# Feed-forward heads over two pairs of row blocks, projection tails by token thirds, and three operand sums on GpSimd

## The reference, cut to what matters

```python
x = x + mix
h = rms_norm(x, norm_ffn[layer])
proj = einsum('btd,df->btf', h, w_in)             # 1024 -> 2 x 2816
a, gate = proj[..., :D_FF], proj[..., D_FF:]
full = concatenate([conv_hist, a], axis=1)
conv = conv_b + sum(full[:, j:j + T] * conv_w[j] for j in range(3))
y = einsum('btf,fd->btd', gelu(conv) * gate, w_out)   # 2816 -> 1024
x = x + y
```

## Time and profile before

| | us |
|---|---|
| median of 3 runs (lowest, highest) | 2767.11 (2763.37, 2767.15) |
| the profiled execution's own time | 2769.66 |
| its span | 2767.9 |
| TensorE busy | 2653.7 |
| VectorE busy | 1843.3 |
| ScalarE busy | 935.5 |
| GpSimd busy | 397.6 |

### The profile page before, as it was taken

One profiled execution on the slowest core, in us unless ns is written; L12 is line 12 of the kernel. 1 busy time (PEld: TensorE's weight loads), 2 busy tenths in 40 slices (PEclk: granted clock), 3 DMA queues, 4 the chain that ended last, 5 costly groups with the idle time before them and its releaser, 6 DMA issues.

```text
span 2767.9 us, 45361 instructions
## 1 busy us (share of the span) xinstructions
PE 2653.7 (96%) x17812; PEld 2579.9 (93%) x17812; DVE 1843.3 (67%) x3057; ACT 935.5 (34%) x1546; POOL 397.6 (14%) x303
## 2 busy tenths in 40 slices
PE   9999999699999998999999999999599999999997
PEld 8989999599999998999888999999599999999997
DVE  3658983687677777789223754454777777777787
ACT  4424462333232233345222112113432222333343
POOL 3234325101010110000001230012101111110000
PEclk9999999799999999999999999999799999999999
DMA  4111001222222338533111111111222222348533
GB/s 149 38 35 54 24 24 38 102 64 72 72 81 69 109 126 288 189 123 118 36 61 50 35 43 42 42 42 34 99 68 91 64 81 72 107 140 291 172 126 126
DMA packets 232449, 248.98 MB, mean 90 GB/s; under 512 B 13051, under 2 KB 170436, under 8 KB 232004
## 3 DMA queue, kind: packets, MB, share of 16 engines
q1 hardware_dynamic: 232228, 246.36, 27.2%
q10 hardware_dynamic: 32, 0.01, 0.0%
HBM read 202.12 MB, written 44.20 MB: 89 GB/s over the span
## 4 chain that ended last, share of the span: by engine, by line
PE 84%; DVE 9%; issue 3%; DMA 2%; ACT 1%; SPq 0%; DVEq 0%; POOL 0%; POOLq 0%; ACTq 0%
PE banks L1420 34%; PE banks L1453 14%; PE banks L917 10%; PE banks L1495 7%; PE banks L942 5%; PE banks L1073 3%; PE banks L1359 2%; PE banks L966 2%; DMA fraw<-in_w_out_ffn 1%; PE banks L1108 1%; PE banks L1011 1%; DVE xs L2076 1%; DVE xs L2229 1%; PE banks L1555 1%; DVE qsc L1734 1%
## 5 line engine op out<-in xcount | busy, mean ns | idle before, releaser
L1420 PE MATMUL banks<-cx,fh 128*128 128x288 f32 x2816 | 497.0, 299 | 44.0 <-DVE cx L2103 33.7
L1420 PEld LDWEIGHTS banks<-cx,fh 128*128 128x128 f32 x2816 | 419.3, 192 | 48.8 <-ACT cx L2978 26.2
L1420 PE MATMUL banks<-cw,fh 128*128 128x288 f32 x2112 | 364.2, 294 | 2.1 <-DVE cw L2103 2.1
L1420 PEld LDWEIGHTS banks<-cw,fh 128*128 128x128 f32 x2112 | 307.7, 188 | 2.5 <-issue 2.5
L1420 PE MATMUL banks<-cx,fl 128*128 128x288 f32 x1408 | 305.8, 298 | 0.0
L1453 PE MATMUL banks<-ysh,fh 128*128 128x288 f32 x1232 | 267.7, 299 | 21.0 <-DVE ysl L2209 20.4
L1453 PE MATMUL banks<-ysh,fl 128*128 128x288 f32 x1232 | 266.5, 298 | 0.0
L1453 PE MATMUL banks<-ysl,fh 128*128 128x288 f32 x1232 | 265.8, 297 | 0.0
L3410 POOL TENSOR_TENSOR gate<-gate,cv 128x1152 f32<-128x1152 f32 x44 | 119.9, 2725 | 953.9 <-DVE gate L2128 788.7
L1420 PEld LDWEIGHTS banks<-cx,fl 128*128 128x128 f32 x1408 | 229.9, 192 | 0.0
L1420 PE MATMUL banks<-cw,fl 128*128 128x288 f32 x1056 | 225.6, 294 | 0.0
(11 more groups left out here) (382 smaller groups left out, 5371.3 us busy)
## 6 DMA issues: line engine op xcount, KB each, us to landing
fraw<-in_w_out_ffn SPq DMA_DIRECT2D x264, 256.0 KB, 3.2
fraw<-in_w_in_ffn SPq DMA_DIRECT2D x176, 256.0 KB, 4.0
y_scratch<-gate SPq DMA_DIRECT2D x44, 576.0 KB, 2.8
raw<-in_w_uv_c SPq DMA_DIRECT2D x64, 256.0 KB, 2.8
yb<-y_scratch SPq DMA_DIRECT2D x10, 1440.0 KB, 9.3
raw<-in_w_in_ab SPq DMA_DIRECT2D x40, 256.0 KB, 2.9
x_scratch<-xs SPq DMA_DIRECT2D x16, 576.0 KB, 7.2
xs<-x_scratch SPq DMA_DIRECT2D x4, 2304.0 KB, 12.1
```

The source lines that it names most:

```text
L1420: mm = pe.matmul(bank[:, M0 + c * CH:M0 + (c + 1) * CH], w[:, pos % RING, k * P:(k + 1) * P], x[:, m, part, c * CH:(c + 1) * CH], start=fi ...
```

## The change

- **Tail by thirds.** Planes 6 and 7 in layer 0, planes 4 to 7 in layer 1 are computed third by third (`by_token_block`). Their weight parts lie in `tw_h`, `tw_l` (freed space), their squares in eight places `sq_t`. `norm_block` 0 stands before the last group of the second third, 1 after the first group of the last third, 2 after the first head product; blocks 1 and 2 take the last plane's square by a second matmul without the GpSimd sum.
- **Head over two pairs.** Pairs 0 and 1 run side by side, q = 1, 2, 3, 7, 5, 6, 4 for both, in four bank pairs, with new places `p1b`, `d1`, `a1`. VectorE's and ScalarE's orders are written out anew; weight sums are formed in place. Step 0's convolution comes at products 13 to 16.
- **Residual later.** Stores of the tail planes are split: first two thirds, then the last. `xs` planes 0 to 3 are read back at down steps 13 and 15 instead of 10; `yb12` is read at steps 22 and 26 instead of 13 and 15, `yb21` at 34, 38, 40 instead of 24, 26, 28. SP's queue issues the weight blocks of pairs 0 and 1 and the stores before the small history loads.
- **Turn to down.** The low parts of steps 0 and 1 come before the last eviction, and the last three convolution parts come in steps 1 to 3; the last gelu comes at step 4 instead of 2.
- **Sums on GpSimd.** `y_sum` for q = 1, 6, 7 (33 of 55 steps a layer) is done by GpSimd after its last `y_prod`; q = 3, 4 stay on VectorE.

```diff
-PLAN.add("abo", 16, 24, 32)
+PLAN.add("abo", 16, 24, 30)
...
+        HEAD = tuple((n, q) for q in (1, 2, 3, 7, 5, 6, 4) for n in range(2))
...
+                sp.wait_ge(acc_free, g0 + NTB * first + 2 * (KD - first))
+                for d in range(first, KD):
+                    sp.dma_start(xscr[l][d][:, 0:2 * TB], xs[:, d, 0:2 * TB]).then_inc(x_moved, 16)
+                sp.wait_ge(acc_free, g0 + NTB * KD)
+                for d in range(first, KD):
+                    sp.dma_start(xscr[l][d][:, 2 * TB:TOK], xs[:, d, 2 * TB:TOK]).then_inc(x_moved_late, 16)
...
-                    if r == 10:
-                        sp.wait_ge(x_moved, 160 * l + 144)
-                        sp.dma_start(xs[:, 0:4, :], xscr[l][0:4].rearrange("d p t -> p d t")).then_inc(x_moved, 16)
+                    if r in (13, 15):
+                        d = r - 13
+                        sp.wait_ge(x_moved, 176 * l + 144)
+                        sp.dma_start(xs[:, d:d + 2, :], xscr[l][d:d + 2].rearrange("d p t -> p d t"))\
...
-                    if r in (13, 15):
-                        a, b = ((0, 6), (6, 11))[r // 15]
+                    if r in (22, 26):
+                        a, b = ((0, 6), (6, 11))[r // 26]
                         y_tiles(yb12[:, a:b, :], a, b, T2S, y_back[1])
-                    if r in (24, 26):
-                        a, b = ((0, 5), (5, 10))[r // 26]
+                    if r in (34, 38):
+                        a, b = ((0, 5), (5, 10))[r // 38]
                         y_tiles(yb21[:, a:b, :], STEPS + a, STEPS + b, T1S, y_back[0])
-                    if r == 28:
...
+            def by_token_block(l, group, ssq):
+
+                first = TAIL_D[l]
+                for tb in range(NTB):
+                    for d in range(first, KD):
+                        if tb == 1 and d == KD - 1:
+                            norm_block(l, 0, ssq)
+                        group(d, tb)
+                        if tb == 2 and d == first:
+                            norm_block(l, 1, ssq)
+
+            def norm_block(l, tb, ssq):
+
+                k = 1 + 2 * l
+                bank = ps[6 + (tb == 0)][:, 0:TB]
+                pe.wait_ge(ssq_added, tail_added(l, tb))
+                if tb == 2:
+                    pe.wait_ge(rms_ready, NTB * k + 2)
+                mm = pe.matmul(bank, ones[:, :], ssq[:, tbs(tb)], start=True, stop=tb == 0)
+                if tb:
+                    s = tail_square(l, KD - 1, tb)
+                    pe.wait_ge(square_ready, TAKEN_SQ[l] + s + 1)
+                    mm = pe.matmul(bank, ones[:, :], sq_t[:, s % 8, :], start=False, stop=True)
+                mm.then_inc(norm_mm, 1)
+
             def norm(k, ssq, blocks=range(NTB)):
 
-                pe.wait_ge(ssq_added, SQUARES[k])
...
+            for u in range(2, 6):
+                abo_unit(n0 + 2 * u, g0 + 3 * u, n0 + 2 * u, g0 + 3 * u)
+
+            def abo_group(d, tb):
+
+                e = 18 + 2 * tb + d - 6
+                acc_bank(g0 + e, g0 + e)
+                for h, (rh, rl) in enumerate(((oh, ol), (ph, pl))):
+                    pe.wait_ge(w_high_ready, n0 + 2 * d + h + 1)
+                    pe.wait_ge(w_low_ready, n0 + 2 * d + h + 1)
+                    for k in range(4):
+                        for c, (w, r) in enumerate(((tw_h, rh), (tw_h, rl), (tw_l, rh))):
+                            mm = pe.matmul(ps[(g0 + e) % BANKS][:, 0:TB], w[:, 2 * (d - 6) + h, k * P:(k + 1) * P],
+                                           r[:, k, tbs(tb)], start=h == k == c == 0, stop=h == 1 and k == 3 and c == 2)
+                mm.then_inc(pe_tick, 1)
+            by_token_block(0, abo_group, ssq_e)
...
+                def head_product(pos):
+
+                    n, q = HEAD[pos]
+                    pe.wait_ge(f_high, done + pos + 1)
+                    pe.wait_ge(f_low, done + pos + 1)
+                    if q == 1:
+                        pe.wait_ge(acc_free, g0 + 20 + 2 * n)
+                    if q == 2:
+                        pe.wait_ge(up_act_out, head_act(l, n, "p1"))
+                    if q == 3:
+                        pe.wait_ge(acc_free, g0 + NTB * KD)
+                        if n:
+                            pe.wait_ge(rms_ready, NTB * (2 + 2 * l))
+                            pe.wait_ge(convc_ready, l + 1)
+                    if q == 7:
+                        pe.wait_ge(up_act_out, head_act(l, n, "c11"))
+                    if q == 5:
+                        pe.wait_ge(up_act_out, head_act(l, n, "e3"))
+                    if q == 6:
+                        pe.wait_ge(up_dve_out, head_dve(l, n, "d"))
+                    if q == 4:
+                        pe.wait_ge(up_dve_out, head_dve(l, n, "c22"))
+                    passes(pos, psp[n + (2 if q in (3, 5) else 0)], q, q in (1, 3, 7, 5))
+
...
+                turn_taps()
+                for pos in range(14):
+                    head_product(pos)
+                    if pos == 0:
+                        norm_block(l, 2, ssq_b if l else ssq_e)
+                for n in range(2, PAIRS):
                     for j in range(7):
                         product(n, j)
...
+                def at_first(tb, d0, d1):
+
+                    for d in range(d0, d1):
+                        (down_tail if l else abo_tail)(d, tb)
...
+                dve.wait_ge(rstd_ready, NTB * 2 * l + 2)
+                dve.wait_ge(x_moved, 176 * l + 16 * KD)
                 for d in range(4):
                     normed(d, T1S)
+                at_first(2, KD - 1 - l, KD - 1)
+                combo_low(0, 0)
+                combo_low(0, 1)
+                at_first(2, KD - 1, KD)
+                combo_low(0, 2)
+                combo_low(0, 3)
+                normed(4, T1S)
+                normed(5, T1S)
+                combo_low(2, 0)
+                normed(6, T1S)
+                combo_low(2, 1)
+                normed(7, T1S)
+                combo_low(2, 2)
+                combo_low(2, 3)
+                up_low(3)
+                dve.wait_ge(rstd_ready, NTB * (1 + 2 * l))
+                dve.wait_ge(x_moved_late, 96 if l else 32)
+                for d in range(4, KD):
+                    normed(d, T2S)
+                dve.wait_ge(convc_mm, l + 1)
                 for k in range(4):
+                    combo_low(6, k)
+                up_sum(4)
+                up_low(4)
+                for d in range(4):
+                    normed(d, T2S)
+                combo_sum(4, 2)
+                up_sum(5)
+                up_low(5)
                 for k in range(4):
+                    combo_sum(3, k)
+                for k in range(4):
+                    combo_low(3, k)
+                for pos in (6, 7):
+                    up_sum(pos)
+                    up_low(pos)
+                for k in (0, 1, 3):
+                    combo_sum(4, k)
+                for k in range(4):
+                    combo_sum(1, k)
+                for k in range(4):
+                    combo_low(4, k)
+                for n in range(2):
+                    head_evict(n, "d")
+                    up_low(8 + n)
+                for k in range(4):
+                    combo_sum(5, k)
+                for k in range(4):
                     combo_low(1, k)
+                for n in range(2):
+                    head_evict(n, "a")
+                    up_low(10 + n)
+                for k in range(4):
+                    combo_low(5, k)
+                up_low(12)
+                up_low(13)
                 dve.memset(apad_a[:, 0:2], 0.0)
                 dve.memset(apad_b[:, 0:2], 0.0)
+                up_evict(10)
...
                     j, kk = divmod(r, STEPS)
                     q = DOWN_ORDER[j]
-                    if q not in SUMMED_Y:
+                    if q not in SUMS_ON_DVE:
                         return
-                    if kk == 0 and q == 1:
-                        dve.wait_ge(y_back[0], 64 * l + 16)
-                        dve.wait_ge(y_back[1], 64 * l + 32)
-                        dve.wait_ge(y_back[2], 48 * (l + 1))
-                    elif kk == 0:
+                    if kk == 0:
+                        dve.wait_ge(ys_summed, 5 * STEPS * l + sums_of(r, SUMMED_Y) - 1)
                         dve.wait_ge(y_back[q == 3], 64 * (l + 1))
                     a, b = Y_PARTS[q]
                     dve.wait_ge(f_done, done + UPS + r - 3)
                     dve.tensor_tensor(yslf[:, r % RINGD, :], y_block(a, kk), y_block(b, kk),
-                                      ALU.subtract if q in (3, 4) else ALU.add)\
...
 
                 w_low(0)
                 y_low(0)
+                w_low(1)
+                y_low(1)
                 up_evict(UPS - 1)
                 w_sum(2)
-                w_low(1)
-                y_low(1)
-                conv_part(STEPS - 1, 1, 2)
-                conv_part(STEPS - 1, 1, 3)
+                conv_part(STEPS - 1, 1, 1)
...
+                def y_sum(r):
+
```

(17 more changed lines are left out.)

659 lines of the change are left out of this document (416 added, 243 removed).

## The result

| | before | after |
|---|---|---|
| median (lowest to highest), us | 2766.42 (2763.37 to 2767.15, 4 runs) | 2727.56 (2725.89 to 2731.69, 4 runs) |
| ratio, 95% interval | | 0.9864 [0.9847, 0.9881] |
| profiled execution: span, its own time | 2767.9, 2769.66 | 2726.6, 2728.34 |

The account below looks back on a forecast made before the run. TensorE, busy 96% of the span, was taken as the bound, with gains only where it starves: 2769.7 - 32 - 20.5 - 1 + 11 = 2727.2, less 2.55 for the timed median, said as 2725; 8-in-10 range 2706 to 2755.

Parts of the forecast that it names:

- The head, layer 0: Start of the up products: loss of 25.5 us in place of 41.0, so 15.5 us gained; 16.5 in layer 1.
- The ledger of VectorE's instructions: Head: VectorE's instructions added up by their spacing from 506.4 on, giving operand times and pair 1 through at about 572.5.
- Nothing else is on the queue here, so I take it as hidden: Projection tail: residual stores of the first two thirds land in time in layer 0, 1 us late in layer 1.
- the 4.3 us for the convolution and the hand-overs: Head: 2.3 us lost to step 0's convolution and GpSimd's product, plus 2 us for hand-overs.
- 66 to 70: Sign in the trace: us from the last projection matmul to the end of the 14th product.
- Rival B, the clock: Heads: TensorE stays at 1.2 GHz, 28 of the 32 us gain are gone, total 2753; chance 0.12.
- The turn, the later reads and the boundaries: Up-to-down turn: 10 us gained in layer 0, 10.5 in layer 1, plus 1 us in all at step boundaries.
- the 5 us a layer for the order of low parts and convolution: Turn to down: low parts ahead of eviction and convolution; of 6.4 us lost, about 1.4 stay.
- Sums on GpSimd: Down products 1, 6, 7: a lock shared with VectorE costs 11 us, bounds 2 and 25.
- 1.88 + 1.43 = 3.31 us of the shared port: Down step with GpSimd sums: 0.14 us over TensorE's 3.175, 0.34 with turn changes, over 66 steps.
- rival A: Down steps with GpSimd sums: the lock costs nothing or its wait is hidden, total 2714; chance 0.15.
- if the down steps with GpSimd sums keep 3.175 us: Sign named in advance, for the down products: the prediction is wrong if this shows, as the no-cost lock rival says.

Follow-up runs that it names:

- the kernel with the stores aside: After's kernel, with SyncE in layer 0 issuing the last two of six residual stores behind the weight blocks, not ahead of them: 2726.4 us, ratio 0.9861.
- the two experiments on VectorE's load: After's kernel with eight more VectorE subtractions in each layer's head: 2740.47 us; with eight scalings there cut from 576 to 32 columns: 2720.60 us.
- two pairs: GpSimd sums against all five products' sums on VectorE: after 2727.6, without 2720.9 us; and both with stores aside, 2726.4 and 2717.9 us.
- `sums_vector`: After's kernel with all five products' sums of y blocks on VectorE again: 2720.87 us, ratio 0.9838.

## Why the prediction was right, point by point

The total was forecast at 2725 and came out at 2727.6. The parts were less good than the sum; that it came so near is in part luck.

**The head, layer 0: 15.5 forecast, 16.6 measured, by two errors that cancel.** The ledger of VectorE's instructions was right where the stores did not disturb it: in the kernel with the stores aside it starts at 506.14 (506.4 forecast) and the 15th product starts at 571.1, where the ledger has pair 1 through at 572.5. In after it starts 3.8 us late, and the 15th product starts at 575.85. The step that failed first stands beside "Nothing else is on the queue here, so I take it as hidden": that sentence asks whether the tail planes' stores land in time, and the six stores of the planes before them, which stand on SyncE's queue ahead of pair 1's weight blocks, have no term at all. They cost the 4.4 us that the edit gives back. The second is the 4.3 us for the convolution and the hand-overs, of which 2.3 were for the convolution after pair 1. From 575.85 to 588.93 four products take 13.1 us, and 4 x 3.175 is 12.7: 0.4 are lost there. **Layer 1: 16.5 forecast, 20.9 measured:** the same 4.3 us, and no late stores, or at least none that delay the norm (TensorE waits 0.23 us for it there).

That VectorE would lead at the third, seventh and fifth products and TensorE in between was half right. The waits ahead of the operands of 3, its partner, 7, 5 and 6 are 2.1, 0.6, 3.9, 1.7 and 1.3 us, where the ledger has 2.7, 2.4, 4, 4.4 and 1.8, and three of them are named to ScalarE. From the last projection matmul to the end of the 14th product it took 61 us where I said 66 to 70: part of VectorE's work was done while the projection, which ended 7.4 us later than the 507.3 that I had kept from before, still ran. And the two experiments on VectorE's load show a pacing engine over the whole stretch, not at three places.

**Rival B, the clock.** The granted clock was 0.50 in two pieces, 532.7 to 536.1 and 543.0 to 549.8, behind or in waits of 2.1 and 3.9 us, and 1.00 between them and from there to the turn; 0.92 over the head. So B did not come. The reason that I gave against it, that at half speed no waits are left, is not shown, since TensorE never stayed there. The clock has a share in the head and is no bound of its own.

**The turn, the later reads and the boundaries: 21.5 forecast, about 12 measured.** Read with the sums on VectorE, from the last up matmul to the end of product 5: 117.3 and 118.3 us before, 112.4 and 111.1 in that kernel, 12.1 us in both layers. The step that failed is the 5 us a layer for the order of low parts and convolution (the 3.04 us gap and the half-speed matmuls): undone, it changes nothing. I had sized a gap by its length and not by what stands behind it. I took the 4.94 us gap as due to late weights and the earlier gap as separate, while the later one takes up whatever the earlier one gives. Near step 8 stands a gap of 2.2 us, where I said under 2. The later reads were right in kind (4.0 and 3.4 us in the first product), and their return in product 1 (2.7 and 1.6 with GpSimd's sums beside it) I had not looked for: 2.4 MB that leave a crowded stretch arrive in another.

**Sums on GpSimd: 11 forecast; measured 6.7 and 8.5 in the medians of two pairs, 10.4 and 9.3 on TensorE's timeline, by another mechanism.** (The spans of the first pair are apart by 7.4, because after was 1.9 us quicker in the up products of layer 0, where the two are the same.) The step that failed is "1.88 + 1.43 = 3.31 us of the shared port", with 0.2 us for the change of turns. The lower bound held: VectorE's three instructions are held for 1.24 us in all, 1.88 + 1.24 = 3.12, the turns cost nothing more, and this fits into 3.175. So the steady steps lose nothing, as rival A said, and the prediction's own sign against its mechanism, "if the down steps with GpSimd sums keep 3.175 us", came true. But A's total (2714) did not come, since the cost lies where VectorE has more to do than three instructions, on TensorE's timeline: product 1 (3.6 and 2.8 us against `sums_vector`; 1.3 in both layers in the kernel before), 0.6 us behind the evictions at the start of each of products 6 and 7, and 1.2 more in product 7 of layer 0 beside the squares. The estimate of 3.13 us a step, from the rule of the Trainium skill (GPSIMD Engine Reference, Elementwise — side-by-side cycle accounting), is right on the steady step to 0.02 us, by luck: the trace has 1.43 us for a sum alone, where the rule gives 1.25, and a hold of 1.24. That the sums would show in products 1, 6 and 7 and not in 5, 3 and 4 was right, for VectorE's durations (up to 1.98 in place of 0.75) and for TensorE's waits, but for 0.4 us in product 5, which `sums_vector` has in layer 1 as well.

**The account.** Forecast -32 - 20.5 - 1 + 11 = -42.5 for the span; measured -41.3, made of -37.5 for the heads (16.6 and 20.9) and -3.8 for the rest. The rest is the 12.1 just told, less the 10.4 for the sums, and 2.3 that nobody forecast: from the last down matmul to the end of the span it takes 25.6 us in before and 25.4 with GpSimd's sums in it, but 23.3 to 23.4 in all kernels with the change, though the change does not touch the code there. Why is open (the parts add up to 4.0, 0.2 off). The heads were worth 5.5 more than I said and all the rest together 6.7 less. The result was near the forecast because of this balance; the mechanism of the heads, which carries it, is shown.

## What to carry to other kernels

Before a gap in a trace is counted as gain, look at who is late behind it: bringing the 3 us gap back cost nothing, since the weights set the pace. When a store or load is moved on an in-order queue, price what is queued behind it first: with two of six stores behind four weight blocks and the others further ahead, the head of layer 0 was 4.4 us shorter. Moving work off a busy engine to one that holds it up did not pay where the busy engine was not the bound: all five sums back on VectorE were 6.7 us faster. And time a stage by the engine that bounds it: evictions, which VectorE runs, put half a microsecond into the wrong products.
